# Spreading gate, gating-input and q/k/v projections over the waits of the recurrent stage of a hybrid encoder kernel

## The reference, cut to what matters

```python
proj = h @ w_in                      # one projection, 12,768 columns
p_r, p_m, p_d, p_g = split(proj)     # RWKV, Mamba (z | xbc | dt), attention (q | k | v), 3 gates
y_r = rwkv7_branch(p_r)              # recurrence over 16 heads x 64, both directions
y_m = mamba2_branch(p_m)             # conv, chunked scan, then y * silu(z), group norm
y_d = diff_attention_branch(p_d)     # 8 heads, two softmax maps each
g = sigmoid(p_g).reshape(..., 3, 1024)
merged = g[0] * (y_r @ w_br_r) + g[1] * (y_m @ w_br_m) + g[2] * (y_d @ w_br_d)
return merged @ w_out
```

## Time and profile before

| | |
|---|---|
| median of 3 runs | 4095.6 us (4091.55 to 4100.12) |
| time of the profiled execution | 4095.83 us |
| its span, first to last instruction | 4094.1 us |
| TensorE busy | 3148.2 us (77% of the span) |
| VectorE busy | 1540.4 us (38%) |
| ScalarE, GpSimd busy | 373.5 us, 219.8 us |
| mean granted TensorE clock | 0.839 of full |
| recurrent stage, each layer | 455.8 and 454.7 us |

### The profile page before, as it was taken

The page is one execution under the profiler, slowest core; times in us unless marked ns, Lnnn a source line. Parts: engine busy times, 40 slices in busy tenths (PEclk is TensorE's granted clock), DMA queues, the critical chain, the costliest instruction groups (busy, mean ns, idle before and its releaser), DMA issues.

```text
span 4094.1 us, 49411 instructions
## 1 busy us (share of the span) xinstructions
PE 3148.2 (77%) x21757; PEld 2243.5 (55%) x21757; DVE 1540.4 (38%) x2580; ACT 373.5 (9%) x764; POOL 219.8 (5%) x354
## 2 busy tenths in 40 slices
PE   5998677779655688679989895776796457877798
PEld 4767455664543436347757584655545334454476
DVE  4522665651236502412034236565502364033201
ACT  0001111100111100200000011001001110011000
POOL 5000000000001000010000000000000010000000
PEclk9999777889875589789989896877897756987899
DMA  7853100003211033055459340000042211321343
GB/s 275 327 185 100 53 6 6 6 2 126 99 67 52 31 125 123 26 182 185 154 200 334 123 141 10 6 4 6 2 147 82 73 52 41 125 103 62 103 154 113
DMA packets 216535, 410.47 MB, mean 100 GB/s; under 512 B 6632, under 2 KB 101414, under 8 KB 216320
## 3 DMA queue, kind: packets, MB, share of 16 engines
q1 hardware_dynamic: 206240, 378.81, 26.3%
q0 software_dynamic: 10080, 28.49, 2.2%
HBM read 406.10 MB, written 1.18 MB: 99 GB/s over the span
## 4 chain that ended last, share of the span: by engine, by line
PE 63%; DVE 20%; issue 8%; DMA 4%; ACT 3%; POOL 1%; DVEq 0%; SPq 0%; POOLq 0%; ACTq 0%
PE ps L822 61%; DVE scratch L1518 8%; DVE scratch L1524 5%; DVE scratch L1521 3%; DMA ring<-in_ffn_w 1%; DMA scratch<-acs_scratch 1%; DMA ring<-in_w_in 1%; ACT scratch L1436 1%; DVE merged L1717 1%; ACT scratch L1303 1%; DVE hT L1521 1%; DVE scratch L1731 0%; PE ps L1172 0%; PE ps L1230 0%; DVE x L1518 0%
## 5 line engine op out<-in xcount | busy, mean ns | idle before, releaser
L822 PE MATMUL ps<-scratch 64*64 64x64 f32 (+5 forms) x14112 | 1222.3, 287 | 402.2 <-DVE scratch L1518 150.0
L822 PEld LDWEIGHTS ps<-scratch 64*64 64x64 f32 (+2 forms) x14112 | 851.6, 162 | 752.7 <-DVE scratch L1518 209.1
L822 PE MATMUL ps<-hT,ring 128*128 128x256 f32 (+1 forms) x4992 | 1126.0, 388 | 50.5 <-DVE hT L1521 31.0
L822 PEld LDWEIGHTS ps<-hT,ring 128*128 128x128 f32 (+1 forms) x4992 | 971.5, 195 | 214.4 <-DVE hT L1521 33.1
L1518 DVE TENSOR_TENSOR scratch<-scratch,ps 128x512 f32<-128x512 f32 (+3 forms) x312 | 201.9, 647 | 1191.0 <-ACT scratch L1313 671.4
L822 PE MATMUL ps<-ring,hT 128*128 128x512 f32 x896 | 410.4, 620 | 29.8 <-DMA ring<-in_w_in 15.8
L1518 DVE TENSOR_TENSOR scratch<-scratch 128x512 f32<-128x512 f32 (+5 forms) x452 | 302.8, 670 | 61.2 <-DMA scratch<-acs_scratch 22.2
L822 PEld LDWEIGHTS ps<-ring,hT 128*128 128x128 f32 x896 | 177.7, 200 | 256.2 <-issue 222.2
L822 PE MATMUL ps<-ring,scratch 128*128 128x512 f32 x512 | 221.7, 592 | 0.0
L1524 DVE SCALAR_TENSOR_TENSOR scratch<-ps,prm,scratch 128x254 f32<-128x254 f32 x192 | 92.6, 482 | 234.8 <-ACTq L1439 228.3
L1524 DVE SCALAR_TENSOR_TENSOR scratch<-scratch,ccol 128x1024 f32<-128x1024 f32 x126 | 164.2, 1303 | 4.5
(11 more groups left out here) (207 smaller groups left out, 1367.3 us busy)
## 6 DMA issues: line engine op xcount, KB each, us to landing
ring<-in_w_in SPq DMA_DIRECT2D x56, 2048.0 KB, 7.8
ring<-in_ffn_w SPq DMA_DIRECT2D x88, 1024.0 KB, 10.0
scratch<-in_ada_w SPq DMA_DIRECT2D x36, 2048.0 KB, 14.2
scratch<-in_ffn_w SPq DMA_DIRECT2D x44, 1024.0 KB, 5.0
ring<-in_w_branch_mamba SPq DMA_DIRECT2D x8, 2048.0 KB, 8.3
scratch<-acs_scratch POOLq DMA_DIRECT2D x32, 512.0 KB, 5.0
ring<-in_w_branch_rwkv SPq DMA_DIRECT2D x4, 2048.0 KB, 7.7
ring<-in_w_branch_diff SPq DMA_DIRECT2D x4, 2048.0 KB, 7.7
```

Of the source, the lines that this page charges most:

```text
L822: return pe.matmul(o, lhsT, rhs, start=start, stop=stop)
```

## The change

Sixteen items per layer (z 4, q and k 4, v 2, gates 6) are taken out of steps 4, 5, 7, 8 and 10 and become IT_FILL, loaded right after IT_RW. Their products are emitted by a generator, one product of 256 columns a step: 16 items x 2 units x 16 steps = 512 steps per layer. A unit is half an item and fills one bank, 1 or 7 by turns. `fill(p, point)` advances the generator at named points, each just ahead of a wait of PE: 80 steps before the first pair (FILL_EARLY) and 54 in each of the eight pairs (FILL_PAIR). To free banks 1 and 7, the pair's v and s and turned outputs move from bank 1 to bank 0, the gate row of a pair from bank 0 to bank 2 as a product of its own (`pair_gate`, at j = 2), and `kk_sum` from banks 4 to 7 to banks 3 to 6.

ACT copies each unit out (identity or sigmoid; for z both) into `stage`, a two-item buffer at the end of the scratch area; POOL multiplies z by its sigmoid. The first 14 items are stored into a DRAM buffer `fill_scratch`, 512 KB each, and SP loads them back ahead of their use: z and the Mamba gates after the first merge, q, k, v at the start of the Mamba branch product, the last gates after it. The two items of the RWKV gates stay in `stage`. `merge` becomes `branch`, with the branch products alone. The first branch's weights are loaded once all 32 units are done. On POOL, `next_pair` waits for `gate_done` in place of `lora_done`.

The core of the diff:

```diff
-IT_FFA, IT_RW, IT_MR, IT_Z, IT_XBC, IT_MM, IT_DF, IT_MD, IT_OUT, IT_FFB, N_ITEM = (
-    0, 11, 19, 23, 27, 33, 39, 45, 49, 51, 62)
+IT_FFA, IT_RW, IT_FILL, IT_BR, IT_XBC, IT_BM, IT_BD, IT_OUT, IT_FFB, N_ITEM = (
+    0, 11, 19, 35, 37, 43, 47, 49, 51, 62)
+FILL_Z, FILL_QK, FILL_V, FILL_GM, FILL_GD, FILL_GR, N_FILL = 0, 4, 8, 10, 12, 14, 16
+FILL_COLS = ([MB0 + 512 * i for i in range(4)] + [DF0 + 512 * i for i in range(6)]
+             + [GT0 + D * b + 512 * h for b in (1, 2, 0) for h in range(2)])
+UNITS, UNIT_STEPS = 2 * N_FILL, 2 * KT
+FILL_BANKS = (1, 7)
+FILL_EARLY = (("vlow", 8), ("vlow_evac", 4), ("vmix0", 4), ("vmix2", 4), ("vmix3", 4), ("kk", 6), ("root", 12), ("rates0", 16), ("rates1", 22))
+FILL_PAIR = (("ops", 12), ("mid", 8), ("lv", 8), ("k0", 2), ("k1", 2), ("k2", 2), ("k3", 2), ("k4", 2),
+             ("r0", 1), ("u0", 1), ("s1", 1), ("r1", 1), ("u1", 1), ("s2", 1), ("r2", 1), ("u2", 1), ("s3", 1),
+             ("r3", 1), ("u3", 1), ("end", 5))
+def filled(p, point):
+    names = [n for n, _ in (FILL_PAIR if p >= 0 else FILL_EARLY)]
+    upto = names.index(point) + 1
+    early = sum(c for _, c in FILL_EARLY)
+    if p < 0:
+        return sum(c for _, c in FILL_EARLY[:upto])
+    pair = sum(c for _, c in FILL_PAIR)
+    return min(early + p * pair + sum(c for _, c in FILL_PAIR[:upto]), UNITS * UNIT_STEPS)
...
+                for i in range(N_FILL):
+                    item = IT_FILL + i
+                    if i < 2:
+                        sp.wait_ge(*group_done(l, group_of(item - 2) + 1))
+                    else:
+                        sp.wait_ge(*fill_done(l, 2 * i - 2))
+                    load(l, item, item % 2, kmaj(w_in[:, :, FILL_COLS[i]:FILL_COLS[i] + 512]))
...
+                sp.wait_ge(*fill_done(l, UNITS))
+                branch(IT_BR, row(a["w_branch_rwkv"], l), 1)
...
+                conv_weights(0)
+                conv_weights(1)
+                sp.wait_ge(*group_done(l, group_of(IT_BR) + 2))
+                for i in range(2):
+                    sp.wait_ge(*z_stored[i](l, 2))
+                    sp.wait_ge(*fill_stored[i](l, 5))
+                sp.dma_start(zy.rearrange("p g t n -> p g (t n)"), stored(FILL_Z, 4)).then_inc(z_loaded.sem, 16)
+                sp.wait_ge(*group_evacuated(l, group_of(IT_BR) + 2))
+                sp.dma_start(stage, stored(FILL_GM, 2)).then_inc(gates_loaded.sem, 16)
...
+                sp.wait_ge(*ymT_ready(l, 4))
+                sp.dma_start(qkT.rearrange("p (g m) s -> p g (m s)", g=4), stored(FILL_QK, 4)).then_inc(qk_loaded.sem, 16)
+                for j in range(2):
+                    sp.dma_start(vdm[:, :, j * 512:(j + 1) * 512],
+                                 fill_dram[FILL_V + j].rearrange("p (t n) -> p t n", t=TT)).then_inc(v_loaded.sem, 16)
+                mamba_weights(1, 0)
+                mamba_weights(1, 1)
+                branch(IT_BD, row(a["w_branch_diff"], l), 1)
+                sp.wait_ge(*group_evacuated(l, group_of(IT_BD)))
+                sp.dma_start(stage, stored(FILL_GD, 2)).then_inc(gates_loaded.sem, 16)
...
+                def z_times_sigmoid(i):
+                    z = stage[:, i % 2, :]
+                    pool.wait_ge(*fill_evac(l, 2 * i + 2))
+                    pool.tensor_tensor(z, z, zsig, ALU.mult).then_inc(z_product.sem, 1)
+                    pool.wait_ge(*z_product(l, i + 1))
+                    pool.dma_start(fill_dram[i], z).then_inc(z_stored[i % 2].sem, 16)
                 pair_loads(0)
+                z_times_sigmoid(0)
+                z_times_sigmoid(1)
                 next_pair(1)
+                z_times_sigmoid(2)
+                z_times_sigmoid(3)
...
+                def fill_products():
+                    for u in range(UNITS):
+                        i, r = u // 2, u % 2
+                        par = (IT_FILL + i) % 2
+                        if r == 0:
+                            pe.wait_ge(*slot_loaded[par](l, loads_before(IT_FILL + i, par) + 1))
+                        if u >= 2:
+                            pe.wait_ge(*fill_evac(l, u - 1))
+                        for h in range(2):
+                            o = ps[:, FILL_BANKS[u % 2], h * S:(h + 1) * S]
+                            for k in range(KT):
+                                if FILL_QK <= i < FILL_V:
+                                    ins = mm(o, slot(par)[:, k, (2 * r + h) * P:(2 * r + h + 1) * P], hT[:, k, :],
+                                             k == 0, k == KT - 1)
+                                else:
+                                    ins = mm(o, hT[:, k, r * P:(r + 1) * P], slot(par)[:, k, h * S:(h + 1) * S],
+                                             k == 0, k == KT - 1)
+                                if h and k == KT - 1:
+                                    ins.then_inc(fill_done.sem, 1)
+                                yield
+                products = fill_products()
+                emitted = [0]
+                def fill(p, point):
+                    while emitted[0] < filled(p, point):
+                        next(products)
+                        emitted[0] += 1
...
                 pe.wait_ge(*kk_sq(l, 1))
                 for n in range(4):
-                    ins = mm(ps[:, 4 + n, :], onesblk[:, :, :].rearrange("p a b -> p (a b)"),
+                    ins = mm(ps[:, 3 + n, :], onesblk[:, :, :].rearrange("p a b -> p (a b)"),
                              kk_sq_buf[:, 2 * n:2 * n + 2, :])
                 ins.then_inc(kk_sum.sem, 1)
+                fill(-1, "root")
                 pe.wait_ge(*kk_root(l, 1))
...
-                    mm(ps[:, 0, 0:S], lora[:, 2, :], cg[:, :], True, False)
-                    mm(ps[:, 0, 0:S], g2b[:, :], cg2[:, :], False, True).then_inc(lora_done.sem, 1)
+                        ins = mm(ps[:, 2 + d, S:2 * S], lora[rr, 1, :], ca[rr, :])
+                    ins.then_inc(lora_done.sem, 1)
+                def pair_gate(q):
+                    pe.wait_ge(*lora_evac(l, q + 1))
+                    mm(ps[:, 2, 0:S], lora[:, 2, :], cg[:, :], True, False)
+                    mm(ps[:, 2, 0:S], g2b[:, :], cg2[:, :], False, True).then_inc(gate_done.sem, 1)
...
+                    if q:
+                        fill(q - 1, "end")
+                    else:
+                        fill(-1, "rates0")
+                        fill(-1, "rates1")
...
+                    fill(p, "ops")
+                    pe.wait_ge(*gate_kept(l, p + 1))
                     pe.wait_ge(*ops_ready(l, p + 1))
...
+                        if k < LV - 1:
+                            fill(p, f"k{k}")
...
+                            fill(p, f"s{j}")
                             pe.wait_ge(*s_evac(l, 3 * p + j))
...
+                        fill(p, f"r{j}")
                         pe.wait_ge(*r_evac(l, 4 * p + j + 1))
...
+                        fill(p, f"u{j}")
                         pe.wait_ge(*u_evac(l, 4 * p + j + 1))
...
+                        if j == 2 and not last:
+                            pair_gate(p + 1)
...
+                pe.wait_ge(*fill_evac(l, UNITS))
...
+                def fill_evacuate(u):
+                    i, r = u // 2, u % 2
+                    dst = stage[:, i % 2, r * 512:(r + 1) * 512]
+                    src = ps[:, FILL_BANKS[u % 2], :]
+                    act.wait_ge(*fill_done(l, u + 1))
+                    if r == 0 and 2 <= i < FILL_QK + 2:
+                        act.wait_ge(*z_stored[i % 2](l, i // 2))
+                    elif r == 0 and i >= 2:
+                        act.wait_ge(*fill_stored[i % 2](l, i // 2 - 2))
+                    if i < FILL_QK:
+                        if r == 0 and i:
+                            act.wait_ge(*z_product(l, i))
+                        own.step(act.activation(dst, src, ACT.Identity))
+                        act.activation(zsig[:, r * 512:(r + 1) * 512], src, ACT.Sigmoid).then_inc(fill_evac.sem, 1)
+                    elif i < FILL_GM:
+                        act.activation(dst, src, ACT.Identity).then_inc(fill_evac.sem, 1)
+                    else:
+                        act.activation(dst, src, ACT.Sigmoid).then_inc(fill_evac.sem, 1)
+                    if r == 1 and FILL_QK <= i < FILL_GR:
+                        act.wait_ge(*fill_evac(l, u + 1))
+                        act.dma_start(fill_dram[i], stage[:, i % 2, :]).then_inc(fill_stored[i % 2].sem, 16)
...
+                    act.wait_ge(*gate_done(l, q + 1))
+                    act.activation(gate[:, q % 2, :], ps[:, 2, 0:S], ACT.Identity).then_inc(gate_kept.sem, 1)
...
-                merge(IT_MM, zy.rearrange("p g t c -> p (g t c)").rearrange("p (k s) -> p k s", s=S), 2)
-                for i in range(0, 2):
-                    for j in range(2):
-                        project(IT_DF, 2 * i + j, i, j, to_channels)
-                for j in range(2):
-                    project(IT_DF, 4 + j, 2, j, to_tokens)
-                pe.wait_ge(*group_evacuated(l, group_of(IT_DF) + 6))
```

(39 more changed lines are left out.)

184 lines of the change are left out of this document (97 added, 87 removed).

## The result

The kernel after the change takes 3742.4 us (median of 4 runs, 3737.9 to 3743.9) against 4096.3 us before: a ratio of 0.9135, 95% interval 0.9119 to 0.9151, so 8.6% faster. I had forecast 3756 us with a range of 3660 to 3900; the profiled execution has a span of 3740.6 us.

What follows compares the result with a forecast made beforehand. TensorE was busy for 77% of the span, with gaps and a 0.80 clock in the recurrent stage. Per layer -232.0 + 21.6 + 26 + 14 = -170, two layers -340, from 4095.8 to 3756 us; range 3660 to 3900.

Steps and rivals of the forecast that it cites:

- The pair: Pair of heads at clock 1.00, 54 steps put into it: +2.7 us per pair, 21.6 per layer.
- changes of tile shape: Steps inserted between 64x64 tiles: 0.25 us per place on the path, 3.3 us per pair, bounds 0 and 7.6.
- mid: Operand products of direction 0 take 3.0 us, not 6.01, and 8 steps fit the 4.16 us gap: -2.6 us per pair.
- (b): Before pair 0, ACT's fifth unit copy and the gate row's copy behind it wait for POOL's product: 5 us per layer.
- (c): POOL's last z product, its store and the next pair's loads delay pair 0's group norm root: 2 us per layer.
- (a): Before the first pair, 8 steps and ACT's copies delay the first mix of v: 3 us per layer.
- (d): The first branch's weights, asked for only after the last unit, come late: 4 us per layer.
- Clock half won: Rival: blocks before the levels still see clock 0.50 in half the pairs; +17 us per pair, 3932 us, chance 0.13.
- Slower: Rival: clock 0.50 all through the stage, levels too; +41 us per pair, 4322 us, chance 0.05.
- Helpers' chain: Rival: PE waits for unit copies, as ACT waits for POOL's products or stores; 34 us per layer, 3824 us, chance 0.13.
- Better hiding: Rival: pairs stay at 58 us, as more small products get shorter at clock 1.00; 3660 us, chance 0.12.
- Nothing hides: Rival: all 23.2 us of steps are added to a pair and the clock returns nothing; 4032 us, chance 0.05.

Runs made afterwards that it cites:

- block of 54: The kernel after, with all 54 steps of a pair in one block ahead of the levels: 3973.8 us, ratio 0.9697.
- runs with dummies: The kernel before, with products without use in the two long stands: 10 and 8 of them 4044.1 us, 6 and 6 of them 4025.2 us.
- run with four more places: The kernel after, with the two steps of each of levels 0 to 3 parted into two places: 3763.3 us, ratio 0.9192.
- runs with empty stands: The kernel after, with steps moved ahead of the levels: from the two long stands 3917.9 us, all 54 3973.8 us, the recurrence's eleven singles 3790.7 us.

## Why the prediction was right

The mechanism came out as forecast: the filled stands bring the clock back, the steps hide in them in part, and each place costs something. That the time came within 14 us was in part luck, since terms that were off by up to 9 us per layer cancelled (*The sum*, below).

**Removed work: -232 per layer, measured -235.1** (the last four rows of the table). The price of 13.75 us per group held. Of the 2.1 us more in the third merge 1.6 lie behind the branch product: the 16 transposes there took 3.52 us before and 1.97 after.

**A step, 0.43 us.** In the block of 54 it is 0.44. Held.

**The pair: forecast +2.7 and 3.3 for changes of tile shape, 6.0; measured +5.7 (63.42 against 57.7).** By parts, from the starts in both traces, for the pair of 57.74 us that begins at 581.13 and the one of 63.42 that begins at 602.69: end of the last chunk to operand products +1.3 (forecast 1.9, and 0.25 for the place); these and mid -2.6 (-2.6 and 0.25); direction 1 and the block ahead of the levels +0.4 (-0.2 and 0.25); levels +4.9 (3.6 and 5 x 0.25 = 4.85); recurrence +1.8 (0 and 1.25). The last was the weak one: eleven singles at 0.63 us do not all hide. The runs with dummies say what such a sum hides: with filled stands and no useful work a pair is 53.2 us, so the clock gives back 4.5 us, and the 54 steps then cost 10.2 us of their 23.2.

**The first pairs.** The first pair of a layer went from 50.30 to 63.73 us, +13.4. I had not read this pair: in the kernel before it waits only 0.76 us ahead of direction 1, whose products take 3.28 us. Those of direction 0 took 5.68 us, but with dummies, where they take 3.29, the pair is still 49.9 us, so there was little to give back. That I had put 13 us on it (6.0, and 7 for the waits (b) and (c)) is a chance hit: the waits did not come. It is the reason why the pairs of a layer came to 53.4 us more (47.6 and 5.8) where 48 were forecast.

**The change of tile shape.** I took 0.25 us, between 0 and 0.36. Measured: 0.20 us on TensorE for a single step among 64x64 tiles, and 0.34 in a level where VectorE's hand-over is pushed back with it. The row that I had drawn the upper bound from was near in part by luck: its 1.22 us hold the end of the last record too. Straight ahead of the dummies the same product takes 1.01 us from start to start (634.97 to 635.98), only 0.15 more than the 0.86. The Trainium skill (TensorEngine Tiling (Array Packing), Key Properties) says that a change of tiling mode drains TensorE; the run with four more places agrees, +1.36 us per pair.

**The once-per-layer waits: forecast 14, measured about 5.** (a) Mix of v: 1.6 for 3. But the traces of the kernel after and of its variants, which are alike up to there, have this start from 472.6 to 475.2, and the kernel before and the ones with dummies from 473.65 to 475.1: the 1.6 is not clear of scatter. (b) This was the step that failed, in size and in place. POOL's product takes 2.50 us, not 4.2 to 8.5; ACT does wait for it, but TensorE does not wait for ACT, since the twelve steps ahead of the operand products last longer:

```profile
476.87 2.50 POOL L780 TENSOR_TENSOR scratch<-scratch 128x1024 f32<-128x1024 f32 x1 [17.47 <-ACT scratch L1495]
476.89 5.45 PE L901 MATMUL ps<-ring,hT 128*128 128x256 f32 x24
479.49 0.60 ACT L1494 ACTIVATE scratch<-ps 128x512 f32<-128x512 f32 x1 [2.71 <-POOL scratch L780]
480.61 0.38 ACT L1557 ACTIVATE scratch<-ps 128x256 f32<-128x256 f32 x1
482.27 1.92 PE L901 MATMUL ps<-scratch 64*64 64x192 f32 x30
```

This is the timeline around pair 0 in the kernel after, which answers to the earlier trace rows: the gate row is copied by 480.99, and PE comes from its steps straight into the operand products at 482.27. (c) Nothing: the second pair has the length of the first. (d) 3.2 us for 4, measured by its removal; both halves' loads landed in 10.7 us.

**The sum.** Per layer I had 9 us too much for the waits, 3 too little for the removed work, and 6 too little for the pairs: 6 to 7 us too much, twice, which is the 14 us between 3756 and 3742.

**The rivals.** *Clock half won* and *clock 0.50 all through* (*Slower*, whose own terms add up to 4319 and not 4322) are out: the clock is 1.00 in the mean of the stage and in each window above. The Trainium skill (TensorE: Matmul & The Clock Gate, A second HAM failure mode) tells of a kernel that cycled through PSUM banks and made the clock swing; with two banks by turns and stands of at most 0.75 us in a pair no such swing shows here. But the rival's mechanism is real, as the runs with empty stands show: 0.54 to 0.65 behind stands of 4 to 6 us, 0.50 behind 2.37 us. *Helpers' chain*: ACT waited once per layer, for 2.71 us, off the path. *Better hiding*: pairs at 58 us would have needed the levels to hide their steps; they cost full price. *Nothing hides*: 13 of 23 us do, against the pair with dummies.

Attention follows the Mamba branch directly, as expected, but only with its first scores, at 1462.78. Then TensorE waits 6.11 us for VectorE, where it waited 3.08 before. The trace shows with what VectorE is late: from 1463.03 it multiplies and adds the second half of the merge (two products of 128x1024, 1.22 us each), then does the work for lambda, and takes up the scores at 1467.73, 4.95 us behind their start, where it was 2.04 before (1612.69 to 1614.73). I had counted 1.4 us of hand-over and 1 us for lambda, which with the 3.08 makes 5.5 us, not 6.11. From the Mamba merge to the third merge the sum is still as forecast (-122.8 for -122.0).

## What to carry to other kernels

A stage in which TensorE hands small products to and fro with another engine has two reserves, its stands and the clock that these cost. Price both apart: fill the stands with dummies, and what the kernel gains is the clock's share (here 4.5 of 57.7 us per pair, for six products in each of two stands). Then put work into the stands by their length, most into the longest, ahead of the wait and not behind it, in few places; each further place cost 0.2 to 0.34 us here beside the work. And read a wait on a DMA against the next wait behind it: of 4.82 us only 3.2 could be had.

## What was unexpected of the hardware

- A 128x1024 product of two float tiles on POOL took 2.34 to 2.50 us, where a 128x256 copy took 1.06.
- In one variant two of sixteen pairs lost some 3 us each: PE stopped for 1.58 and 1.65 us with nothing that it waited for in the trace, and the granted clock was lower behind the stop.
- A stand of 2.35 us in the recurrence, between small products, was enough for the granted clock to go from 1.00 to 0.50 (kernel before, 633 to 637).
- Granted clock behind a stand is not one value: the same operand products took 4.95 us at 0.64 behind 3.83 us of idle time and 5.79 at 0.54 behind 4.14 us in one run, and 5.00 at 0.63 behind 5.94 us and 4.94 at 0.65 behind 4.14 us in another.
